# Token sums ahead of the norm's factor, fifteen more chunks in seven products, and an interleaved tail

## The reference

```python
def swiglu(x, w_gate, w_up, w_down):
    return (jax.nn.silu(x @ w_gate) * (x @ w_up)) @ w_down
x = x + 0.5 * swiglu(rms_norm_2(x, ffn1_norm[layer]), ...)
```

## Time and profile before

| | |
|---|---|
| runs, median (lowest to highest) | 2720.7 us (2720.49 to 2720.86), 3 runs |
| the profiled execution | 2721.14 us |
| its span | 2719.3 us |
| granted TensorE clock | 1.00 |
| PE busy | 2701.3 us (99%) |
| PEld busy (weight loads, beside the matmuls) | 2381.9 us (88%) |
| DVE busy | 2054.4 us (76%) |
| ACT busy | 1052.6 us (39%) |
| POOL busy | 493.8 us (18%) |
| DMA | 266.22 MB, mean 98 GB/s |

### The profile page before, as it was taken

How to read it: one execution, slowest core, us unless ns; L and a number is a source line. 1 busy time by engine, 2 the same in 40 slices (tenths; PEclk the granted TensorE clock), 3 DMA queues, 4 the chain that set the end, 5 groups by cost and what they waited for, 6 DMA issues and landing times.

```text
span 2719.3 us, 38909 instructions
## 1 busy us (share of the span) xinstructions
PE 2701.3 (99%) x15824; PEld 2381.9 (88%) x15824; DVE 2054.4 (76%) x2044; ACT 1052.6 (39%) x1147; POOL 493.8 (18%) x298
## 2 busy tenths in 40 slices
PE   9999999999999999999999999999999999999999
PEld 7978789888999889998768899988999988889998
DVE  5778766457899789886576888868888665688884
ACT  4333534444344463333363433335333322243332
POOL 0124014031000241002222200023000142510000
PEclk9999999999999999999999999999999999999999
DMA  4221133312323323223301232233232323222332
GB/s 169 80 76 63 48 111 124 107 68 90 108 95 107 112 90 109 102 101 110 114 33 63 93 109 96 107 109 109 94 108 94 111 105 104 98 93 94 109 109 93
DMA packets 39761, 266.22 MB, mean 98 GB/s; under 512 B 4528, under 2 KB 5808, under 8 KB 8240
## 3 DMA queue, kind: packets, MB, share of 16 engines
q1 hardware_dynamic: 38016, 259.02, 27.1%
q10 hardware_dynamic: 1584, 4.87, 0.5%
HBM read 261.77 MB, written 2.10 MB: 97 GB/s over the span
## 4 chain that ended last, share of the span: by engine, by line
PE 94%; DVE 3%; POOL 1%; ACT 1%; issue 1%; DMA 0%; SPq 0%; DVEq 0%; POOLq 0%; ACTq 0%
PE ps L2041 29%; PE ps L2042 29%; PE ps L2043 29%; PE ps L2274 1%; PE ps L2340 1%; PE ps L2371 1%; DVE w_lo L1041 1%; PE ps L2662 1%; PE ps L2634 1%; PE ps L2296 1%; POOL up_b L1902 0%; PE ps L2354 0%; ACT w_hi L527 0%; PE ps L2646 0%; POOL ssum L1896 0%
## 5 line engine op out<-in xcount | busy, mean ns | idle before, releaser
L2041 PE MATMUL ps<-x_hi,w_hi 128*128 128x512 f32 (+1 forms) x1736 | 615.4, 354 | 2.2 <-DVE w_lo L1225 1.5
L527 ACT ACTIVATE w_hi<-stage 128x2048 fp32r<-128x2048 f32 (+1 forms) x241 | 416.2, 1727 | 519.0 <-PE ps L2043 516.6
L2043 PE MATMUL ps<-x_hi,w_lo 128*128 128x512 f32 (+1 forms) x1736 | 605.3, 349 | 0.0
L2042 PE MATMUL ps<-x_lo,w_hi 128*128 128x512 f32 (+1 forms) x1736 | 605.2, 349 | 0.0
L1041 DVE TENSOR_TENSOR w_lo<-stage,w_hi 128x2048 fp32r<-128x2048 f32 (+1 forms) x241 | 505.2, 2096 | 56.4 <-ACT w_hi L527 56.4
L2041 PEld LDWEIGHTS ps<-x_hi,w_hi 128*128 128x128 f32 x1736 | 328.8, 189 | 47.5 <-issue 3.6
L2042 PEld LDWEIGHTS ps<-x_lo,w_hi 128*128 128x128 f32 x1736 | 328.9, 189 | 43.5 <-issue 3.6
L2043 PEld LDWEIGHTS ps<-x_hi,w_lo 128*128 128x128 f32 x1736 | 328.7, 189 | 42.6
L1930 POOL TENSOR_TENSOR up_b<-up_b,gate_b 128x1024 f32<-128x1024 f32 x50 | 119.9, 2397 | 1302.1 <-PE ps L2043 1145.3
L2041 PE MATMUL ps<-f_hi,w_hi 128*128 128x512 f32 x880 | 342.8, 390 | 0.0
L2042 PE MATMUL ps<-f_lo,w_hi 128*128 128x512 f32 x880 | 342.8, 390 | 0.0
(11 more groups left out here) (442 smaller groups left out, 4976.9 us busy)
## 6 DMA issues: line engine op xcount, KB each, us to landing
stage<-in_stream SPq DMA_DIRECT2D x242, 1024.0 KB, 4.8
h<-in_x ACTq DMA_DIRECT2D x2, 1024.0 KB, 5.4
out_x<-h SPq DMA_DIRECT2D x8, 256.0 KB, 2.1
h<-in_x SPq DMA_DIRECT2D x6, 256.0 KB, 3.7
mem_raw<-in_mem ACTq DMA_DIRECT2D x1, 1024.0 KB, 4.9
stage<-in_stream SPq DMA_DIRECT2D x6, 128.0 KB, 4.1
h<-in_x SPq DMA_DIRECT2D x1, 512.0 KB, 6.1
mask_f<-in_constants ACTq DMA_DIRECT2D x1, 448.0 KB, 6.2
```

What stands on the lines that cost most here:

```text
L527: act.activation(w_hi[slot][:, 0:width], stage[slot][:, 0:width], ACT.Copy).then_inc(hi_ready, 1)
L2041: pe.matmul(out_ap, wh, xh, start=first, stop=False)
L2042: pe.matmul(out_ap, wh, xl, start=False, stop=False)
L2043: return pe.matmul(out_ap, wl, xh, start=False, stop=last)
```

## The change

- `SEVENS`: in FFN 1 to 4 gate 1, up 1 and up 10 join the seven-product chunks, in FFN 0 gate 2, up 2 and up 10. 98 chunks in place of 83.
- `token_sums` and `tokens_scaled` (before `t_half`) stand ahead of the norm's root and reciprocal, on VectorE and on ScalarE. In FFN 1 to 4 the weight sums of gate 1, its `s_hi` and `s_lo` stand there too, and two of four `t_lo`; the other two follow gate 0's evacuation. `t_x` lies elsewhere; up 1 has its own `s_hi1`, `s_lo1`; the copy of the first product has storage of its own.
- Up 10: VectorE combines, then multiplies with the gate itself; the gate was multiplied with `rstd` before.
- `TAIL`: the tail's first two chunks are interleaved by hidden tile, so that the last step's hidden tiles are asked for later.
- `BESIDE`: the product of up 1 (GpSimd) waits for gate 2's end in FFN 1 to 4. In FFN 1 the second statistic's matmul moves from behind gate 1 to behind up 0.

```diff
-SEVENS = [{"gate": range(3, STEPS), "up": range(3, STEPS - 1)}] + 4 * [{"gate": range(2, STEPS), "up": range(2, STEPS - 1)}]
+SEVENS = [{"gate": range(2, STEPS), "up": range(2, STEPS)}] + 4 * [{"gate": range(1, STEPS), "up": range(1, STEPS)}]
...
+        first = place("first", take(4 * HALF), [P, HALF])[:, :]
...
-        T_SUMS = [2, 0, 0, 0, 0]
-        T_ROUND = [3, 1, 1, 1, 1]
+        TAIL = [(0, (16, 17, 18, 19)), (1, (16, 17)), (0, (20, 21)), (1, (18, 19, 20, 21)), (2, range(LAST_K, FT)), (3, range(LAST_K, FT))]
+
+        BESIDE = [[None if it == 0 or i == 0 and it < 2 else ("gate", 2) if it == 1 else ("down", it - 2) for it in range(STEPS - 1)] for i in range(5)]
...
+            def tokens_scaled(i):
 
                 for k in range(KT):
                     act.activation(t_x[:, k, :], h[:, k, :], ACT.Copy, scale=pc(GAIN[i], k)).then_inc(t_scaled, 1)
+                if (i, 2) in NTH:
+                    sums_hi(i, 2)
+                for q, done in zip(T_ORDER, (2, 3, 3, 4)):
+                    act.wait_ge(t_sum, 4 * i + done)
+                    act.activation(t_hi[:, q, :, :], t_f[:, q, :, :], ACT.Copy).then_inc(t_rounded, 1)
...
             residual("a_out")
+            tokens_scaled(2)
             stat(NS0["a_out"])
-            t_half(2)
             ffn(2)
...
             def token_sums(i):
 
+                if (i, 2) in NTH:
+                    weight_sums(i, 2)
...
                 dve.tensor_tensor(t_f[:, T4, :, :], x21, t_f[:, T2, :, :], ALU.subtract).then_inc(t_sum, 1)
+                if (i, 2) in NTH:
+                    sums_lo(i, 2)
+                token_lo(i, 0)
+                token_lo(i, 1)
...
                     else:
+                        combined(i, p)
+                        ffn_lo(i, p + 2)
                         dve.wait_ge(f_ready, past(f))
+                        dve.wait_ge(rescaled, RESCALED[i])
                         for e in range(2):
-                            if i == 0:
-                                dve.wait_ge(silu_ready, f + 2)
-                            dve.tensor_tensor(up_b[:, e, :], ps[:, two_banks(p) + e, :], rstd[:, :], ALU.mult).then_inc(acc_evac, 1)
+                            dve.tensor_tensor(up_b[:, e, :], free(blocks[:, 2 * e, :], 0, [[1, S]]), gate_b[:, e, 1:1 + S], ALU.mult).then_inc(acc_evac, 1)
...
+                    if p == 0:
+                        token_lo(i, 2)
+                        token_lo(i, 3)
...
+                    if (kind, it) == ("gate", STEPS - 1):
+                        dve.wait_ge(silu_ready, f + 2)
+                        dve.tensor_tensor(gate_b[:, :, 1:1 + S], gate_b[:, :, 1:1 + S], free(rstd[:, :], 0, [[0, 2], [1, S]]), ALU.mult).then_inc(rescaled, 1)
...
             residual("a_out")
+            token_sums(2)
             norm_rstd(NS0["a_out"])
             ffn(2)
...
-                for j in range(4):
+                for j, tiles in TAIL:
                     c, t = C0[name] + j, T0[name] + 2 * j
-                    pe.wait_ge(lo_ready, c + 1)
-                    pe.wait_ge(acc_evac, t - 2)
-                    for k in range(LAST_K, FT):
-                        if j == 0:
-                            pe.wait_ge(f_ready, past(FT * i + k + 1))
+                    if tiles[0] == LAST_K:
+                        pe.wait_ge(lo_ready, c + 1)
+                        pe.wait_ge(acc_evac, T0[name] - 2 if j < 2 else T0[name])
+                    for k in tiles:
+                        pe.wait_ge(f_ready, past(FT * i + k + 1))
```

More of the change, by code:

```diff
@@ L191, in build @@
         t_f = place("t_f", hid(24), [P, 4, KP, HALF])
-        t_x = place("t_x", hid(32), [P, KT, S])
+        t_x = place("t_x", hid(8), [P, KT, S])
         s_hi = place("s_hi", hid(32), [P, 4 * KP * P], F32R)
@@ L394, in build, with summed_at @@
         S_FIRST = {at: n for n, at in enumerate((i, p) for i, p in SEVEN_ORDER if ORDER[p][0] == "gate")}
-        first = ssum[:, 0:HALF]
+        def summed_at(p):
+            return (s_hi1, s_lo1) if ORDER[p] == ("up", 1) else (s_hi, s_lo)
         def chunk_at(i, p):
@@ L535, in ffn_hi, with sums_hi @@
                     return
-                n = NTH[i, p]
                 if kind == "up":
                     split_hi((c, 0), SINGLES)
[L539 to L544, removed]
+                if p != 2:
+                    sums_hi(i, p)
                 if kind == "gate":
                     split_hi((c, 0), SINGLES)
+            def sums_hi(i, p):
+                c, n, kind = C0[f"up{i}"] + p, NTH[i, p], ORDER[p][0]
+                act.wait_ge(s_sum, 4 * n + 4)
+                if kind == "gate" and p > 2:
+                    act.wait_ge(chunk_done, c - 1)
+                elif (i, p - 1) in S_FIRST and ORDER[p][1] > 1:
+                    act.wait_ge(s_used, S_FIRST[i, p - 1] + 1)
+                act.activation(summed_at(p)[0][:, :], s_f[:, :], ACT.Copy).then_inc(s_rounded, 1)
             def first_product(i, p):
@@ L600, in ffn @@
                     f = FT * i + 2 * it
-                    if i == 1 and (kind, it) == ("gate", 1):
-                        stat(NS0["renorm"])
+                    if i == 1 and (kind, it) == ("up", 0):
+                        stat(NS0["renorm"], 3)
                     if kind == "down":
@@ L605, in ffn @@
                     ffn_hi(i, p + 2)
[L606 to L609, removed]
+                    if kind == "gate" and it and BESIDE[i][it - 1] == (kind, it):
+                        hidden_hi(i, it - 1)
                     if kind == "gate":
@@ L1052, in ffn_lo, with sums_lo @@
                     split_lo((c, 0), SINGLES)
-                dve.wait_ge(s_rounded, NTH[i, p] + 1)
-                dve.tensor_tensor(s_lo[:, :], s_f[:, :], s_hi[:, :].bitcast(F32), ALU.subtract).then_inc(s_ready, 1)
+                if p != 2:
+                    sums_lo(i, p)
                 if kind == "gate":
                     split_lo((c, 0), SINGLES)
+            def sums_lo(i, p):
+                hi, lo = summed_at(p)
+                dve.wait_ge(s_rounded, NTH[i, p] + 1)
+                dve.tensor_tensor(lo[:, :], s_f[:, :], hi[:, :].bitcast(F32), ALU.subtract).then_inc(s_ready, 1)
             def weight_sums(i, p):
@@ L2076, in some, with stat @@
                     mm.then_inc(chunk_done, 1)
-            def stat(n):
+            def stat(n, bank=4):
                 pe.wait_ge(ss_ready, 9 * n)
-                pe.matmul(ps[:, 4, :], ones, ssum[:, :], start=True, stop=True).then_inc(stat_done, 1)
+                pe.matmul(ps[:, bank, :], ones, ssum[:, :], start=True, stop=True).then_inc(stat_done, 1)
             def both():
@@ L2132, in summed @@
                 def summed(q):
-                    return lambda j: (s_hi[:, (KP * q + j) * P:(KP * q + j + 1) * P], s_lo[:, (KP * q + j) * P:(KP * q + j + 1) * P])
+                    hi, lo = summed_at(p)
+                    return lambda j: (hi[:, (KP * q + j) * P:(KP * q + j + 1) * P], lo[:, (KP * q + j) * P:(KP * q + j + 1) * P])
                 def tokens(k, half):
@@ L2181, in ffn @@
                     elif (i, p) in NTH:
+                        if i == 1 and (kind, it) == ("up", 1):
+                            pe.wait_ge(std_ready, NS0["renorm"] + 1)
                         seven_products(i, p, kind)
```

85 lines of the change are left out of this document (42 added, 43 removed).

## The result

The changed kernel takes 2761.48 us, the median of 4 runs (2759.68 to 2761.84), and the kernel before takes 2720.78 beside it: 1.0148 times as long, 95% interval 1.0136 to 1.016. It is slower, and 6.5 us above the predicted 2755. The profiled run took 2761.77 us with a span of 2760.0; the mean granted clock is 0.992.

A forecast was written before the change was run, and what follows sets the result against it. TensorE was taken as the bound, with VectorE's late low halves the risk. FFN 2 to 4 add 17.4 us, FFN 1 13.9, FFN 0 2.5: + 33.8 on 2721.1, forecast 2755, 8-in-10 range 2735 to 2769.

The forecast's parts named there:

- The gain: TensorE, 15 chunks in seven products: 0.83 us saved per conversion, 2.5 a stage, 12.5 together.
- The chain on VectorE: Stage head, x_lo to gate 1's w_lo: 20.4 us plus a 1.15 GpSimd turn against 15.0; gate 1 6.5 late, FFN 2 to 4.
- The clock: TensorE's clock falls in each wait before gate 1 and slows matmuls behind it: 1.8 us a stage, half in FFN 0.
- the 2737 rival: Stage heads: chain late but GpSimd gives way and the clock stays; + 16, 2737 us; 20 in 100.
- The second wait of 0.8: TensorE at gate 2: VectorE needs 21.0 us against two chunks of 10.08; 0.8 us, hidden if the clock falls.
- The rival of 2770: Slow clock lasts, 3.6 rather than 1.8 a stage, and lateness of 1 to 2 us reaches gate 2; 9 in 100.
- FFN 1: Stage FFN 1: gate 1 waits 14.6 us, plus 1.8 clock, less 2.5 gain: 13.9 us longer.
- a net of zero: FFN 1 behind gate 1: covered second statistic's matmul and 0.8 hole cancel up 2 about 1.6 late from the second reciprocal.
- The turns: FFN 1's head: VectorE and GpSimd alternate at the shared port, 8.8 us; 9.7 if every operation waits.
- Taken up by chunk 1's slack: Tail: residuals of tail chunk 0 come 2.7 later, absorbed by chunk 1's slack.
- The tail: Up 10 and tail: hidden tiles ready 6.8 and 7.4 us after up 10, TensorE asks after 8.2; cost 0.
- The rival of a faster kernel: Stage heads: the 20.4 us are not in the way, the 12.5 gain remains, 2708 us; 5 in 100.

The follow-up runs named there:

- experiment 7: Experiment 5 cut to the last up (up 10) in seven products and the interleaved tail, heads as in the kernel before but for `BESIDE`: 2716.76 us.
- experiment 3: Changed kernel with GpSimd's squares and sums for the first block's last norm (head of FFN 1) on 8 of 512 columns: 2750.05 us.
- Experiments 5 and 6: 5: experiment 4 with FFN 1's head as in the kernel before, 2713.46 us. 6: experiment 5 with the tail chunks in their old order, 2719.71 us.
- experiment 4: Changed kernel with gate 1 plain, only the four token sums ahead of the norm, t_hi and t_lo behind w_lo: 2721.88 us.
- experiment 5: Experiment 4 with FFN 1's head as in the kernel before and its up 1 plain, last up in seven: 2713.46 us.

## Why the prediction was right, and where its sizes were off

**The gain.** 0.83 us a conversion was right: experiment 7 gives 0.81, and the stages of the changed kernel close with 2.5 each.

**The chain on VectorE.** The main step, and it held: 20.4 for the list (20.3 in experiment 3) and one turn of 1.15 gave 6.5 us; the waits are 6.45, 6.51 and 6.45. The turn is in the first s_f, 1.78 in place of 0.68, as predicted (a reading of the row: no run took GpSimd's work out of that head). FFN 0's 4.1 came as 3.96.

**The clock.** It fell in or just behind every wait before gate 1, as the forecast had it and the 2737 rival did not. The term was mis-sized: 1.8 us a stage, measured some 2.0 to 2.7, and 1.7 in place of 0.9 in FFN 0. I took the start's short stretch of 3.6 us as the model. Behind FFN 0's wait the slow matmuls did run 3.6 us, so halving the term there was wrong; in FFN 1 to 4 they ran 4.2 to 5.9. With it FFN 2 closes: 6.45 + 2.6 - 2.5 = 6.55 against 6.75. The second wait of 0.8 is really hidden by it, shown by the 1.06 that appears once the clock stays up. The rival of 2770 had the mechanism of the longer slow clock, but not its other half: nothing was handed on to gate 2.

**FFN 1.** Predicted +13.9, measured +17.6, the largest miss. Gate 1 began 15.9 us later into the stage than before (38.97 against 23.08) in place of 14.6; behind gate 1 the forecast had a net of zero and the trace 1.9; the clock took 0.5 more. The terms one by one:
- The turns cost 10.6, not 8.8; x_lo ended 0.6 earlier in the stage, so 1.2 of the 1.8 reached gate 1. I had let three sums pass GpSimd because they do at 1547.00; here none passed, and the first three s_f took 1.75 to 1.79 each. Beside them GpSimd's timeline has this row, and two of its later ones:

```profile
965.72 3.42 POOL L1942 TENSOR_TENSOR up_b<-up_b,sq_b 128x512 f32<-128x512 f32 x2
...
976.67 1.84 POOL L1934 TENSOR_TENSOR sq<-h 128x512 f32<-128x512 f32 x1
978.58 2.16 POOL L1936 TENSOR_TENSOR ssum<-ssum,sq 128x512 f32<-128x512 f32 x1
```

  The Trainium skill, "SBUF — State Buffer", section "SBUF: two separate sides", has the operation that starts first keep the shared port pair until it ends; the trace agrees here, with an s_f of 1.78 beside GpSimd and of 0.68 in experiment 3. The 9.7 by that rule was the nearer figure.
- "Taken up by chunk 1's slack" was wrong. FFN 1's first statistic, which GpSimd sums behind tail chunk 0, made TensorE wait 1.5 us. Experiments 5 and 6 differ in the tail's order alone and show 0.7 us of it with the interleaved tail and 0.15 with the other; the rest appears in experiment 4 too, 1.6, where the token sums stand ahead of the norm as here. In the changed kernel this wait costs nothing extra, because gate 1 then waits for w_lo anyway.
- Behind gate 1 there are waits of 1.5 at up 2, then 0.5 and 1.6. The 1.5 is the late up 2 that the prediction had, from the second reciprocal ahead of its w_lo; the others it lacked. Against the 3.6 stand the hole of 0.8 and the second statistic's matmuls of 0.9, which moved ahead of gate 1: 1.9 and not zero. This is not lateness handed on from gate 1: in experiment 3 gate 1 waits 5.0 us, and the 1.5 and 1.6 are the same. Both w_lo come behind work of the second norm on VectorE, the second behind a product of 4.09 us (2.29 in experiment 5) beside one of GpSimd:

```profile
1024.68 3.35 DVE L1240 RECIPROCAL sq<-ssum 128x512 f32<-128x512 f32 x1
...
1051.15 4.09 DVE L1212 TENSOR_TENSOR h<-h,sq 128x2048 f32<-128x2048 f32 x1
```

  Experiment 5, which puts back FFN 1's order and takes up 1 plain, has none of the three; which of the two does it is not shown.

  Added up, each hole less the normal spacing of the matmuls: 1.64 + 4.96 + 8.35 + 1.52 + 0.51 + 1.56 = 18.5, clock 2.3, less conversions 2.5 and the 0.8 hole of before: 17.5 against 17.6, good to a few tenths (TensorE stood 0.3 at the first statistic before, too). The second statistic's wait of 4.96 is not an extra term: it stands ahead of gate 1, inside the time that gate 1 would wait for w_lo.

**The tail.** Cost 0, right: no hole in any tail, where the order before it would have 1.2 to 1.7. The hidden tiles were ready 6.6 and 7.2 us after up 10 (6.8 and 7.4 predicted). DVE at FFN 2's tail, up 10 having ended at 1842.6:

```profile
1842.80 0.69 DVE L1120 TENSOR_TENSOR blocks<-ps,first 128x512 f32<-128x512 f32 x1 [3.35 <-PE ps L2078]
...
1845.43 1.76 DVE L1056 TENSOR_TENSOR w_lo<-stage,w_hi 128x1536 fp32r<-128x1536 f32 x1
1847.11 1.28 DVE L1228 TENSOR_TENSOR up_b<-blocks,gate_b 128x512 f32<-128x512 f32 x2
1848.49 1.29 DVE L1231 TENSOR_TENSOR f_lo<-up_b,f_hi 128x512 fp32r<-128x512 f32 x2
```

**The sum.** Against the predicted 33.8: FFN 1 3.7 more, FFN 2 to 4 2.1 more together, FFN 0 0.8 more, the start 0.3. That is the distance to 40.7. By stage the misses have one sign, so the total did not come out by errors that cancel. The rival of a faster kernel put its point of decision at a list of 15.0 us; the list was 21.4.

Not settled: why the slow stretch is 10.2 us in FFN 2 and 6.8 in FFN 3 and 4 at waits of the same length (4.3, 2.6 and 1.0 us of it lie in the wait), and why three sums pass GpSimd in one place and none in the other.

## What to carry to other kernels

When work is moved into an engine's idle time, write that engine's list from the last fixed event to the operand that the bottleneck wants, and subtract the time the bottleneck gives: here 15.0 us, and at the head of FFN 2 list minus 15.0 is the wait to 0.1 us in five kernels. The idle time that other engines force on that engine belongs in the list too. A conversion that saves the bottleneck 0.8 us is dear if it adds 4 us to a list with 1 us to spare; the same conversion where the list has room is the whole gain. Fix the stages one by one: FFN 1, with two statistics on GpSimd, alone turned experiment 4's gain into nothing.

## What the runs showed of the hardware

In the changed kernel the granted clock fell to half (1.2 GHz) in waits of 4.8 to 6.5 us, and 0.2 us behind the end of the 4.0 us one in FFN 0. It stayed low while matmuls ran: low for 3.4 us in all in FFN 0, 6.8 in FFN 3 and 4, 10.2 in FFN 2, 17.1 in FFN 1. In the last of these TensorE had two matmuls of the second statistic between waits of 4.8 and 7.5 us and ran them at half, 1.01 us from start to start where experiment 4 has 0.53. In the gate-1-plain kernel a wait of 2.5 us in FFN 4 was followed by no stretch at half clock, nor was experiment 4's of 3.4 us in FFN 1; the one of 3.95 us in FFN 2 was, for 3.4 us from 0.9 us behind its end. Unread matmuls in the wait kept it at 1.00 and gained 6.4 us over five stages. The Trainium skill, "TensorE: Matmul & The Clock Gate", section "What's actually happening", has half rate as the default that activity lifts; the filled waits agree.

In FFN 1 eleven operations of VectorE with both operands in SBUF, beside GpSimd's, took 10.6 us more than in experiment 3 with GpSimd's squares and sums narrow, and GpSimd's own grew as well: a square took 1.84 and a sum 2.16 at 976.67, where the same two took 1.04 and 1.29 in the kernel before. Sharing cost both engines, and so both statistics came late.
